# Three edits at the seams of a two-block forward pass: later row scaling, own gate banks for a second step, earlier squares

## The reference

```python
def first_block(x, ...):                      # D_FF = 2816
    h = rms_norm(x, norm_mix)
    u = h @ w_in                              # 2560 columns: lru_x, lru_g, q, k, v
    y_lru = gelu(lru_g) * rg_lru(causal_conv(lru_x))
    y_att = stick_breaking_attention(q, k, v)
    x = x + concat(rms_norm(y_lru), rms_norm(y_att)) @ w_out
    gu = rms_norm(x, norm_ffn) @ w_ffn_in
    x = x + (silu(gu[:, :D_FF]) * gu[:, D_FF:]) @ w_ffn_out
    return rms_norm(x, norm_final)

def second_block(x, ...):
    proj = rms_norm(x, norm_mix_g) @ w_in     # conv parts, q, k, v, forget logit, gates
    ...                                       # gated convolution, forgetting attention
    x = x + (g_conv * y_conv + g_attn * y_attn) @ w_o
    up = causal_dwconv(rms_norm(x, norm_ffn_g) @ w_up)
    x = x + (silu(a) * b) @ w_down            # a, b = halves of up
    return rms_norm(x, norm_f_g)
```

## Time and profile before

| | |
|---|---|
| time, median of 3 runs | 1336.82 us (1336.48 to 1337.02) |
| time of the profiled execution | 1336.55 us |
| its span | 1334.8 us |
| busy: PE, DVE, ACT, POOL | 1300.6, 824.3, 537.7, 89.5 us |
| mean granted clock of PE | 0.996 of full |
| output transfers at the end | 4, 512 KB each, median 2.6 us from issue to landing |

### The profile page before, as it was taken

How to read it: one execution, slowest core, us unless ns; L and a number is a source line. 1 busy time by engine, 2 the same in 40 slices (tenths; PEclk the granted TensorE clock), 3 DMA queues, 4 the chain that set the end, 5 groups by cost and what they waited for, 6 DMA issues and landing times. The chain is left out here.

```text
span 1334.8 us, 15700 instructions
## 1 busy us (share of the span) xinstructions
PE 1300.6 (97%) x6240; PEld 1059.4 (79%) x6240; DVE 824.3 (62%) x929; ACT 537.7 (40%) x587; POOL 89.5 (7%) x88
## 2 busy tenths in 40 slices
PE   7999999999999999999999999999999999999996
PEld 5777677788888889997888888758888888888774
DVE  6797765833333357878646433557666666677775
ACT  6463663512222235446211322464343333345553
POOL 4003010000000011200000001000310000002020
PEclk9999999999999999999999999999999999999998
DMA  4422101132222359553333322201222222257583
GB/s 163 132 95 68 59 1 63 64 126 94 94 94 94 126 145 257 111 96 111 119 135 95 95 95 95 95 1 60 99 95 95 94 94 94 94 181 128 172 145 92
DMA packets 107716, 139.00 MB, mean 104 GB/s; under 512 B 3482, under 2 KB 80522, under 8 KB 107538
## 3 DMA queue, kind: packets, MB, share of 16 engines
q1 hardware_dynamic: 95826, 113.11, 25.7%
q0 software_dynamic: 11824, 25.18, 10.3%
q10 hardware_dynamic: 16, 0.00, 0.0%
HBM read 136.18 MB, written 2.11 MB: 104 GB/s over the span
## 5 line engine op out<-in xcount | busy, mean ns | idle before, releaser
L1629 PE MATMUL psum<-act_hi,w_hi 128*128 128x512 f32 x1224 | 483.4, 395 | 5.7 <-DVE w_lo L994 2.0
L1631 PE MATMUL psum<-act_hi,w_lo 128*128 128x512 f32 x1224 | 479.6, 392 | 0.0
L1630 PE MATMUL psum<-act_lo,w_hi 128*128 128x512 f32 x1224 | 479.4, 392 | 0.0
L632 ACT ACTIVATE w_hi<-raw 128x2048 fp32r<-128x2048 f32 (+1 forms) x93 | 176.4, 1897 | 531.7 <-PE psum L1631 512.4
L1629 PEld LDWEIGHTS psum<-act_hi,w_hi 128*128 128x128 f32 x1224 | 229.8, 188 | 61.7 <-issue 6.3
L1630 PEld LDWEIGHTS psum<-act_lo,w_hi 128*128 128x128 f32 x1224 | 229.9, 188 | 51.2 <-issue 1.7
L1631 PEld LDWEIGHTS psum<-act_hi,w_lo 128*128 128x128 f32 x1224 | 229.9, 188 | 49.7
L994 DVE TENSOR_TENSOR w_lo<-raw,w_hi 128x2048 fp32r<-128x2048 f32 (+1 forms) x93 | 212.0, 2281 | 62.9 <-ACT w_hi L632 62.9
L1880 PE MATMUL psum<-part_hi,w_hi 128*128 128x256 f32 x308 | 86.7, 282 | 0.0
L1881 PE MATMUL psum<-part_lo,w_hi 128*128 128x256 f32 x308 | 86.0, 279 | 0.0
L1882 PE MATMUL psum<-part_hi,w_lo 128*128 128x256 f32 x308 | 86.0, 279 | 0.0
(11 more groups left out here) (288 smaller groups left out, 1612.1 us busy)
## 6 DMA issues: line engine op xcount, KB each, us to landing
raw<-in_w_in SPq DMA_DIRECT2D x30, 1024.0 KB, 5.2
raw<-in_w_ffn_in SPq DMA_DIRECT2D x22, 1024.0 KB, 5.1
raw<-in_w_up SPq DMA_DIRECT2D x22, 1024.0 KB, 5.1
x_buf<-in_w_ffn_out POOLq DMA_DIRECT2D x6, 1024.0 KB, 10.4
x_buf<-in_w_down POOLq DMA_DIRECT2D x6, 1024.0 KB, 9.4
raw<-in_w_out SPq DMA_DIRECT2D x4, 1024.0 KB, 5.0
raw<-in_w_o SPq DMA_DIRECT2D x4, 1024.0 KB, 5.0
x_buf<-in_w_ffn_out POOLq DMA_DIRECT2D x3, 768.0 KB, 10.5
```

The source lines that it names most:

```text
L632: A(w_hi[:, s % 2, 0:n], home(s, n), ACT.Copy).then_inc(w_hi_ready, 1)
L1629: mm(dst, stationary[0], moving[0], start=first, stop=False)
L1630: mm(dst, stationary[0], moving[1], start=False, stop=False)
L1631: return mm(dst, stationary[1], moving[0], start=False, stop=last)
```

## The change

Three edits.

**1. End of the kernel.** On ACT the scaling of row groups 0 and 1 moves from n = 17, which is ahead of `split_w` of the last slab (n = 18 calls `split_w(S_DOWN2 + 20)`), to behind the loop. On DVE `row_out` of the same groups moves from n = 17 to the end of n = 18, behind the last slab's `split_w`.

```diff
@@ ACT, last product
-                if n == 17:
-                    scale_row(0)
-                    scale_row(1)
+            scale_row(0)
+            scale_row(1)
             for n in range(3):
@@ DVE, last product
                     mark(V.tensor_tensor(xr[1][0], xr[1][0], rest, ALU.subtract))
+                if n == 18:
                     row_out(0)
                     row_out(1)
```

```diff
@@ ACT
+            split_w(S_FFN + 2)
-            root(N_FFN, psum[:, bank_of(GROUP[S_FFN]) + 3])
+            root(N_FFN, psum[:, bank_of(GROUP[S_FFN + 1]) + 3])
...
-            with act.Fori(0, FFN_STEPS - 1) as i:
+            silus(0)
+            split_w(S_FFN + 3)
+            act.wait_ge(ffn_hidden, 2)
+            with act.Fori(1, FFN_STEPS - 1) as i:
@@ DVE
-            add_squares(N_FFN)
+            add_squares((N_FFN,), range(DC))
+            split_w(S_FFN + 2)
             inverse(N_FFN)
...
-            with dve.Fori(0, FFN_STEPS - 1) as i:
+            ffn_step(0, lambda: None, lambda: split_w(S_FFN + 3, 0))
+            ffn_step(1, lambda: split_w(S_FFN + 2, 1), lambda: split_w(S_FFN + 3, 1), 2)
+            with dve.Fori(2, FFN_STEPS - 1) as i:
@@ PE, up()
+                wait_w(s0, 1)
+                if own_banks:
+                    slab_a(s0, i=1, apart=2)
+                    wait_freed(GROUP[s0 + 1])
+                    slab_a(s0 + 1, i=1)
+                    wait_w(s0, 2)
                 wait_freed(GROUP[s0])
-                wait_w(s0, 1)
-                one_column(bank_of(GROUP[s0]) + 2)
-                with pe.Fori(1, FFN_STEPS) as i:
+                one_column(bank_of(GROUP[s0 + 1]) + 2)
+                with pe.Fori(2 if own_banks else 1, FFN_STEPS) as i:
```

```diff
@@ ACT
                 if n in (18, 19):
                     for pos in range(2 * (n - 18), 2 * (n - 18) + 2):
                         mix2_operand(pos)
+                    mix2_squares(n - 18)
             ...
             split_w(S_K2 + 1)
-            for pos in range(DC):
+            for pos in range(2, DC):
                 mix2_squares(pos)
@@ DVE
                         split_act(C_MIX2 + pos, ...)
+                    add_squares((N_FINAL, N_MIX2), range(n - 18, n - 17))
             ...
-            add_squares(N_FINAL, N_MIX2)
+            add_squares((N_FINAL, N_MIX2), range(2, DC))
```

More of the change, by code:

```diff
@@ L1210, in _, with add_squares @@
                 split_w(s + 2)
-            def add_squares(*rs):
-                n = SQ_FIRST[rs[0]]
-                for c in range(DC):
+            def add_squares(rs, some):
+                n = SQ_FIRST[rs[0]] + len(rs) * some[0]
+                for c in some:
                     for r in rs:
@@ L1225, in add_squares, with ffn_step @@
                         n += 1
-            add_squares(N_FFN)
+            add_squares((N_FFN,), range(DC))
+            split_w(S_FFN + 2)
             inverse(N_FFN)
-            def ffn_step(i, next_gate, next_up):
+            def ffn_step(i, next_gate, next_up, apart=0):
                 finished(S_FFN, i)
                 for j in range(2):
-                    V.tensor_tensor(tmp[:, j], bank(S_FFN, j), R(N_FFN), ALU.mult).then_inc(ffn_gate, 1)
+                    V.tensor_tensor(tmp[:, j], bank(S_FFN, j + apart), R(N_FFN), ALU.mult).then_inc(ffn_gate, 1)
                 next_gate()
@@ L1639, in act_part, with slab_a @@
                 return act_hi[:, chunk, t0:t0 + n], act_lo[:, chunk, t0:t0 + n]
-            def slab_a(s, q=None, i=None, part=act_part, order=range(DC), ahead=lambda pos: None):
+            def slab_a(s, q=None, i=None, part=act_part, order=range(DC), ahead=lambda pos: None, apart=0):
                 wait_w(s, i)
-                b = bank_of(GROUP[s])
+                b = bank_of(GROUP[s]) + apart
                 for pos, k in enumerate(order):
@@ L1850, in _, with up @@
             slab_b(S_OUT_ATT + 1, lambda k: act_part(WC + k))
-            def up(s0, q, r, sums_at):
+            def up(s0, q, r, sums_at, sums_bank, own_banks):
                 wait_banks(GROUP[s0])
@@ L1859, in up @@
                 wait_banks(GROUP[s0 + 1])
-                slab_a(s0 + 1, ahead=lambda pos: sum_squares(r, bank_of(GROUP[s0]) + 3) if pos == sums_at else None)
+                slab_a(s0 + 1, ahead=lambda pos: sum_squares(r, sums_bank) if pos == sums_at else None)
+                wait_w(s0, 1)
[4 more added lines that the diff above has]
+                    wait_w(s0, 2)
                 wait_freed(GROUP[s0])
-                wait_w(s0, 1)
-                one_column(bank_of(GROUP[s0]) + 2)
-                with pe.Fori(1, FFN_STEPS) as i:
+                one_column(bank_of(GROUP[s0 + 1]) + 2)
+                with pe.Fori(2 if own_banks else 1, FFN_STEPS) as i:
                     for j in range(2):
@@ L1869, in up @@
                         slab_a(s0 + j, i=i)
-            up(S_FFN, C_FFN, N_FFN, WC)
+            up(S_FFN, C_FFN, N_FFN, WC, bank_of(GROUP[S_FFN + 1]) + 3, True)
             def seven_product(n, k, m):
@@ L2032, in _ @@
             assert bank_of(GROUP[S_DOWN2]) == bank_of(GROUP[S_DOWN]) == 4
-            up(S_UP, C_UP2, N_FFN2, 0)
+            up(S_UP, C_UP2, N_FFN2, 0, bank_of(GROUP[S_UP]) + 3, False)
             pe.wait_ge(up_scaled, 4 * FFN_STEPS - 2)
```

## The result

The changed kernel takes 1326.8 us (median of 4 runs, 1326.24 to 1327.24), the kernel before beside it 1336.92 us (4 runs, 1336.48 to 1337.65). The ratio is 0.9923 with an interval of 0.9906 to 0.9941: faster, by 10.1 us. The forecast was 1327.0.

A forecast was written before the change was run, and what follows sets the result against it. PE bounds the kernel (busy 1300.6 of 1334.8 us), so only its gaps count: 5.85 + 2.65 + 1.3 = 9.8 us off 1336.55 gives 1326.75, expected median 1327.0; 8-in-10 range 1326.0 to 1328.9.

The forecast's parts named there:

- Edit 1: Kernel end: last slab starts 3.29 us earlier and runs at full clock, so the last matmul comes 5.85 us earlier.
- clock low all the same: Rival at the kernel end: PE gets the low clock whatever it does, last-slab edit gives 3.29 us, total 1329.6; chance 0.06.
- the gap of 2.46 us: PE's gap at 266.07, followed by a full-rate stream; taken as support for full clock after a 0.3 us gap.
- Edit 2: Feed-forward's second step: split ahead of root and reciprocal, own banks; stream 3.04 us earlier, less 0.39, net 2.65 us.
- the price of the one-column pair: Feed-forward: the one-column matmuls stand one step later and cost 0.39 us.
- The margins in banks and weights: Feed-forward step 1: weights ready 3 us before PE needs them, banks 2 and 3 free, so PE's stream goes on.
- Edit 3: Squares before S_Q2: four additions leave DVE's chain, which starts earlier after a 1.4 us delay; gain 1.3 us.
- I take no loss: At S_K2+1: the delayed split ends near when PE wants it, 611.08; a possible 0.1 us loss not counted.
- a gap of 0.1 remains: At S_Q2: weight remainder done 1.3 us earlier against PE's bracket of 1.43, leaving 0.1 us.
- the squares give nothing: Rival: the late split of S_K2+1 or a slower hand-over eats the 1.3 us; total 1328.3, chance 0.13.
- The sum: Whole kernel: 5.85 + 2.65 + 1.3 = 9.8 us gained, expected median 1327.0 us.
- The slower rival, the loop's code: First feed-forward loop: shifted code makes each pass wait at the jump; 1340.5 us at 1.5 us a pass, chance 0.03.

The follow-up runs named there:

- squares_only: The kernel before with Edit 3 alone (some squares and additions moved to n = 18 and 19); 1335.51 us, ratio 0.9985.
- act_half: The changed kernel with row_out of groups 0 and 1 back ahead of DVE's last remainder, ACT's scaling left late; 1330.03 us, ratio 0.9949.
- one_row: The changed kernel with only row_out(0) back at n = 17 and row_out(1) still at n = 18; 1327.56 us, ratio 0.9931.
- the two experiments: The changed kernel with the second gate slab's split back behind root and reciprocal, 1330.3 us; or with step 1 sharing step 0's banks, 1328.36 us.
- again: The changed kernel measured once more, unchanged; 1326.88 us, ratio 0.9926.
- adds_later: The changed kernel with DVE's two additions of n = 19 moved behind the split of S_K2+1; 1327.18 us, ratio 0.9922.
- banks_only: The kernel before with Edit 2 alone (early split on both engines, peeled steps, other pair of banks); 1333.62 us, ratio 0.997.
- tail_only: The kernel before with Edit 1 alone (scaling and row_out moved behind the last split); 1331.52 us, ratio 0.9955.
- shifted: The changed kernel with five one-column memsets of unused scratch added on DVE at n = 13; 1326.17 us, ratio 0.9924.
- shifted_later: The changed kernel with five added DVE memsets and the two additions of n = 19 behind the split of S_K2+1; 1327.16 us, ratio 0.9926.

## Why the prediction was right, step by step

**Edit 1, predicted 5.85 us.** Right in mechanism and size: 5.84 in PE's starts, both together with the other edits and alone, and 5.5 alone by the medians. DVE was next to be late, as said, with a gap of 0.26 where 0.2 to 0.4 stood in the text. The clock stayed full, so the first rival ("clock low all the same") fell. But the reason I gave for it was weak. I took the stretch behind the gap of 2.46 us as a sign that such a gap does no harm. In squares_only the same gap is followed by a clock of 0.71 and steps of 0.42 us, and act_half fell after 1.97 us. PE's timeline and the stretch in squares_only:

```profile
265.66 0.35 PE L1687 MATMUL psum<-ident 128*128 128x1 f32 x2 [2.46 <-DVE w_lo L995]
...
267.72 0.63 PE L1631 MATMUL psum<-act_hi,w_hi 128*128 128x512 f32 x1
```

```profile
265.66:269.20 3.54, 3.54 (x12) 2.85 (x13) 3.54 (x5) 0.11 (x1) 0.00 (x0) 0.71 0.68 217
```

What held was the size of the new gap, 0.26 us. one_row shows that 1.13 us at this place left the clock full as well, so the forecast had room, though the record before did not show it.

**Edit 2, predicted 2.65.** In the traces 2.82. The earlier start was worked out to the digit (3.04); the term that was off is the price of the one-column pair, taken as 0.39 from the earlier trace rows and 0.22 at its new place. The margins in banks and weights were as worked out: both halves are needed, as the two experiments show. Alone it gave 3.4 (2.7 to 5.5) by the medians. 0.36 more come from the pause that the peeled code moved out of the chain before S_Q2, and 0.25 are lost to the pause in the second attention. The rest fits the clock, which was higher in four of its nine runs than in any run before; that the edit is the reason is not shown.

**Edit 3, predicted 1.3.** 1.06 in the trace, 1.3 in the traces of squares_only and again, 1.5 (0.8 to 3.2) alone by the medians. Here one step failed: "I take no loss" at S_K2+1. Everything ahead of that split moved by 1.77 us instead of 1.4 (606.32 + 2.68 against 607.23), because of the pause, so it came 0.37 us later than I had it. PE waited 0.19 and took 0.59 instead of 0.23 us from the last matmul of one slab to the first of the next. The sentence before had named the place, with a price of 0.1; it was 0.36. It cost nothing that adds_later could win back, since S_Q2's weights bound PE anyway, and "a gap of 0.1 remains" there came out as none. The rival ("the squares give nothing") isn't borne out: the interval of squares_only leaves out zero.

**The sum, predicted 9.8.** In the two profiled executions it is 9.3, mainly because two losses had no term: 0.30 at the late slab of `w_ffn_out` and 0.26 in the second attention. The first differs between executions of the same kernel: in again no such time is lost. The medians differ by 10.1. So that the median came within 0.2 us of the forecast is in part luck: the profiled execution after the change is the slowest of its four.

**The slower rival, the loop's code.** It fell: PE's table of waits shows no gap that comes once a pass, and banks_only is faster. Yet its mechanism has a small relation on another engine: a pause at a place in the code, below. The Trainium skill, Runtime: NRT & Kernel Launch, Instruction fetch mechanics, tells of code brought in by blocks with a cost that is mostly hidden. For PE's loops the trace agrees: no gap shows. On DVE a pause of 0.46 to 0.48 us goes with a transfer of instructions, as the last section shows, so there a cost of that kind isn't hidden.

## What to carry to other kernels

Follow a wait to what stands ahead of it in the program of the engine that is late, and ask there whether that work is wanted by anyone yet: both large gains here are orders of two things on one engine. When a wait has two conditions, work out when each is met; moving one buys only the distance to the other. A gap in a dense stream can cost most of its own length again in clock: 2.5 us behind one of 3.57 at the end, 1.55 behind one of 1.97 there, 1.6 behind one of 2.46 in mid-kernel in one trace of three. A gap that is only made shorter can keep the clock's share: at the end the clock fell with 1.97 us left and not with 1.13.

## What was not expected of the hardware

**The clock falls in some executions and not in others.** The same gap of 2.46 us left it full in two kernels' profiles (the kernel before and tail_only) and not in a third's (0.71 in squares_only). It can also fall far from any edit: in the second attention squares_only has 0.56, adds_later 0.55, and the kernel before 1.00 in the same stage, with the same wait of 0.78 us on PE ahead of it. squares_only first, then the kernel before, which gets 22 matmuls done where the other gets 10:

```profile
864.15:868.00 3.85, 3.85 (x10) 1.86 (x11) 2.79 (x13) 2.72 (x9) 0.00 (x0) 0.56 0.00 0
```

```profile
864.15:868.00 3.85, 3.69 (x22) 2.59 (x22) 2.79 (x13) 2.88 (x10) 0.00 (x0) 1.00 0.00 0
```

By PE's starts such an episode costs 1.6 to 1.7 us, as much as the smaller edits, so one trace against another can mislead: read the clock of both before the difference. When it falls and when not stays open.

**DVE pauses 0.46 to 0.48 us where instructions are brought in.** In the kernel before, tail_only and squares_only the pause is inside the chain, at 615.69, 616.13 and 615.53:

```profile
615.69 6.26 DVE L1223 TENSOR_TENSOR tmp<-tmp 128x512 f32<-128x512 f32 x8 [0.46 <-DVE tmp L1223]
```

With the peeled steps of edit 2 it lies about 14 instructions earlier, at the same instruction in the changed kernel and in again. Five instructions more on DVE, and it doesn't show. The traces also list what the DMA queues moved. One of the two queues of instructions, q14, moves packets of 8 KB (15 packets and 0.12 MB on the page of either kernel). In all nine traces that show this pause, one such packet starts 0.7 to 2.1 us after the pause ends. The view of the queues by window (queue, packets, MB, share) has it in the kernel before in 616.30 to 616.50, in the changed kernel in 601.40 to 602.00, and in shifted already in 596.40 to 596.70, ahead of both additions and while DVE runs a single remainder of 2.29 us:

```profile
q14 instruction: 1, 0.01, 12.5%
...
q14 instruction: 1, 0.01, 3.7%
...
q14 instruction: 1, 0.01, 7.5%
```

The 0.28 us pause in the second attention behaves alike: all eight traces with edit 2 and without the memsets have it, each followed by a packet (0.65 us behind 869.17 in the changed kernel), and shifted and shifted_later don't. So the packet moves with five DVE instructions, and the pause goes with it: it shows in the traces where short operations depend on one another. That it is covered under DVE's long operation in shifted is inferred from the packet's time. By the trace's times the engine doesn't wait for the packet's data, since it runs on before the packet starts. What it does in those 0.5 us stays open.

**A slab can run a little slower.** Behind its late start S_K2+1 takes 0.233 us a step in the changed kernel's profile ((620.03 - 609.07)/47 from the timeline, 0.229 elsewhere). In again, with the same late start, it is 0.229, so the wait isn't the reason; open as well.
